# The delta rule's inverse: the mirrored update of each level by a transpose of the update's copy instead of a third product

## The chip, the cores and the metric

The kernel runs on one core of a Trainium2 chip. Time is device time in microseconds, the median of several executions. PE is TensorE, DVE VectorE, ACT ScalarE, POOL GpSimd, SP SyncE; PSUM is where PE writes, SBUF the working memory.

## What is computed

A stack of layers over 256 tokens with a width of 2048, all in fp32. The third layer has, beside other heads, eight heads of a gated delta rule. Cut to what matters, over the tokens of one head:

```python
kb = kc * bc[..., None]
L = jnp.where(tril & ~eye, jnp.einsum('bhncd,bhnsd->bhncs', kb, kc) * decay, 0.0)
rhs = jnp.concatenate([vc * bc[..., None], kb * jnp.exp(gc)[..., None]], axis=-1)
sol = lax.linalg.triangular_solve(L + eye, rhs, left_side=True, lower=True, unit_diagonal=True)
```

The kernel has no triangular solve. It treats each head as two blocks of 128 tokens, builds the inverse of each unit lower triangular 128x128 block (I + L) by doubling, and uses products with it for the rest. Level 0 is the inverse of the 2x2 blocks on the diagonal, I - L. Each of the levels 1 to 6 joins neighbouring blocks of size w = 2, 4, ... 64: the off-diagonal part is minus (inverse of the later block) times (L between them) times (inverse of the earlier one).

## The kernel before

**Streams.** One program per engine, written out by hand, with semaphores between them. The bulk is projections: weights come by DMA from SP in tiles of 128x2048, each in two pieces of 1024 columns. Each piece is split by ACT (L659, the high part) and DVE (L1487, the low part) into two tiles for which PE has fast passes; PE then multiplies it with the activations. ACT and DVE stay up to four pieces ahead (`ahead`, L444). Other work is written as generators, put in at *ticks* (L426): two for every piece, after its first and its second half. A `yield` ends a step, and `rate` says how many steps there are per tick: 5/6 for half 0 of the delta rule, later 7/8. In ACT's and DVE's programs (`proj`, L459) the split of a piece to come stands before the first tick of each piece. Each engine runs strictly in the order of its program. Evictions of a projection block stand after the last tick of its last piece.

**The delta rule** (`gdn`, one generator per engine, L1198 on ACT, L2325 on DVE, L3242 on PE) runs twice, for the halves H = 0 and 1 of four heads each. The names: `Tm` and `Tt` hold the inverses and their transposes, 512 columns (four heads) for each of two token blocks; `LM` is L with the level's mask, made by POOL (`inverse_masks`, L592); `Mx` holds copies; `DT` (`l3_dt`, 1536 columns) is free scratch by then, `LM` is its first third, `Two` its second.

One level, before:
- lm, PE L3330: four products, LM times the current inverse (a *mixed* view that takes one block of Tm and one of Tt). ACT copies the result to `Mx` (mx, L1273).
- ACT also copies the mixed inverse into `Two` (mix, L1269), after DVE has finished the level before.
- newm, PE L3336: four products Two times Mx. And right behind it new, PE L3340: four products with the operands exchanged, which give the transposed update.
- DVE subtracts newm's result (tn, L2438) and new's (tt, L2445) from the mixed views, straight from PSUM.

The next lm needs tn; the next mix needs tt. In the steps of the generators, lm stands in one step, newm and new in the next. ACT's mix and mx stand in newm's step, ahead of it, and both of DVE's subtractions in the step of the next lm. After level 6 PE makes u0 (L3346), which needs tt6, then lu and u1, a step each. While the inverse of half 0 is built, projection blocks of half 1's inputs run, whose results DVE evicts in pairs (L1708 two reductions, L1713 a product); beside half 1's there is a block evicted by ACT with a change of table (L795).

The transposes that are in this layer already (L3308, L3315) are PE instructions with the identity as moving operand.

Of the kernel before, what the change touches and what calls it, by code (L numbers as in the profile page):

```python
# [11 lines left out]
ACT = mybir.ActivationFunctionType  # L12
# [99 lines left out]
def later(ap, h):  # L112

    return ap.rearrange("p (m n) -> p m n", n=2 * h)[:, :, h:2 * h]
# [6 lines left out]
def mixed(a, b, h):  # L121

    n = a.shape[1]
    return bass.AP(a.tensor, a.offset, [list(a.ap[0]), [2 * h, n // (2 * h)], [b.offset - a.offset + h, 2], [1, h]])
# [12 lines left out]
class Bank:  # L137


    def __init__(self, i, n, t):  # L140
# [5 lines left out]
    "lru_act": ("l1_r", "l1_i", "l1_tanh", "l1_ln", "l1_a", "l1_root", "lam_exp", "lam_ln", "l1_exp"),  # L146
    "gates_act": ("l2_gelu_u", "l2_gelu_v", "l2_silu_g", "gla_gate", "gd_gate", "hg_gate", "hg_sig", "gla_exp", "gla_ln",
                  "hg_ln", "lb_exp"),
    "gdn_act": ("gd_mix", "gd_decay", "gd_ln", "gd_mx", "gd_out", "gd_root", "gd_silu", "gd_sq", "gd_tm", "gd_u", "conv0"),
    "copied_act": ("l2_al", "l3_small", "l4_small", "l4_gl", "cmp_kc", "cmp_silu", "cmp_vc", "small"),  # L150
    "head_squares": ("hn_sq", "gate_sq"),
    "lru_dve": ("l1_conv", "l1_half", "l1_iu", "l1_neg", "l1_scan", "l1_u", "l1_y", "l1_zero", "lam", "lb"),
# [492 lines left out]
class Scalar(Lane):  # L645
# [552 lines left out]
    def gdn(self, H):  # L1198
        m, e = self.m, self.e
        qk, sm, DT, Tm, Tt, U = m.l3_qk, m.l3_sm, m.l3_dt, m.l3_tm, m.l3_tt, m.l3_mx  # L1200
        if H:
            yield from self.conv(1)
        self.silu_part(H, 2)
        yield
        yield
        if H == 0:
            bsv = sm[:, :, 32:48]
            self.wait_ge("small_T")
            b = self.bank("small_T")
            e.activation(bsv, b.t[:, 0:128].rearrange("p (a n) -> p a n", a=2)[:, :, 0:16], ACT.Copy).then_inc(  # L1210
                *self.up("small", 0, frees=[b]))
            self.sq_turned = ("small_T",)
            self.ln_set()
            e.activation(m.cell(8, "ea"), m.c("a_log", 0, 8), ACT.Exp).then_inc(*self.up("small", 1))
            self.wait_ge("small", 0)
            e.activation(sm[:, :, 8:16], bsv[:, :, 8:16], ACT.Exp, scale=-1.0).then_inc(*self.up("small", 2))
            yield
            self.wait_ge("small_v", "abs")
            e.activation(sm[:, :, 16:24], sm[:, :, 16:24], ACT.Exp, scale=-1.0).then_inc(*self.up("small", 3))
            self.wait_ge("small", 3)  # L1220
            e.activation(sm[:, :, 16:24], sm[:, :, 16:24], ACT.Ln, bias=1.0).then_inc(*self.up("small", 4))
        else:
            self.ln_set()
        for hh in range(0, 4, 2):
            yield
        if H == 0:
            yield
            self.wait_ge("small_sum")
            b = self.bank("small_sum")
            e.activation(sm[:, :, 24:32], b.t[:, 0:16].rearrange("p (a n) -> p a n", a=2), ACT.Copy).then_inc(  # L1230
                *self.up("small", 5, frees=[b]))
            yield
        for now in skew(4, 3):
            for s, g in now:
                dst = DT[:, (g % 3) * 512:(g % 3) * 512 + 512]
                if s == 0:
                    x2 = qk[:, 2 * g:2 * g + 2, :].rearrange("p c n -> p (c n)")
                    self.wait_ge("gd_silu", H, g // 2)
                    if g >= 3:
                        self.wait_ge("gd_unit", H, g - 3)  # L1240
                    e.activation(dst, x2, ACT.Square).then_inc(*self.up("gd_sq", H, g))
                if s == 2:
                    self.wait_ge("gd_ss", H, g)
                    b = self.bank("gd_ss", H, g)
                    e.activation(dst, b.t, ACT.Ln, bias=m.cst[:, C_EPS:C_EPS + 1]).then_inc(
                        *self.up("gd_ln", H, g, frees=[b]))
                    self.wait_ge("gd_ln", H, g)
                    e.activation(dst, dst, ACT.Exp, scale=-0.5).then_inc(*self.up("gd_root", H, g))
            yield
        for now in skew(4, 3):  # L1250
            yield
        self.wait_ge("gd_kb", H, 3)
        e.activation(DT, DT, ACT.Exp).then_inc(*self.up("gd_decay", H))
        yield
        for now in skew(8, 2):
            yield
        yield
        for g in range(2):
            self.wait_ge("gd_tT", H, g)
            b = self.bank("gd_tT", H, g)  # L1260
            e.activation(Tm[:, g * 512:(g + 1) * 512], b.t, ACT.Copy).then_inc(*self.up("gd_tm", H, 0, g, frees=[b]))
        for level in range(1, 7):
            yield
            w = 1 << level
            if level == 1:
                self.wait_ge("gd_tm", H, 0, 1)
            else:
                self.wait_ge("gd_tt", H, level - 1)
            e.activation(DT[:, 512:1024].rearrange("p (m c n) -> p m c n", c=2, n=w), mixed(Tm[:, 512:1024], Tt[:, 0:512], w),  # L1269
                         ACT.Copy).then_inc(*self.up("gd_mix", H, level))  # L1270
            self.wait_ge("gd_lm", H, level)
            b = self.bank("gd_lm", H, level)
            e.activation(U[:, 0:512], b.t, ACT.Copy).then_inc(*self.up("gd_mx", H, level, frees=[b]))  # L1273
            yield
        yield
        self.wait_ge("gd_u0", H)
        b = self.bank("gd_u0", H)
        e.activation(U[:, 0:512], b.t, ACT.Copy).then_inc(*self.up("gd_u", H, 0, frees=[b]))
        yield
        yield  # L1280
        self.wait_ge("gd_u1", H)
        b = self.bank("gd_u1", H)
        e.activation(U[:, 512:1024], b.t, ACT.Copy).then_inc(*self.up("gd_u", H, 1, frees=[b]))
        self.f.add("mid")
        yield
        for tt in range(2):
            self.wait_ge("gd_o", H, tt)
            b = self.bank("gd_o", H, tt)
            e.activation(m.l3_vb[:, tt, :], b.t, ACT.Copy).then_inc(*self.up("gd_out", H, tt, frees=[b]))
        yield from self.headnorm(f"gd{H}", m.l3_vb, 4, 128, DT, ("gd_out", H, 1))  # L1290
        self.ends(f"gd{H}")
# [187 lines left out]
class Vector(Lane):  # L1479
# [845 lines left out]
    def gdn(self, H):  # L2325
# [95 lines left out]
                            *self.up("gd_l2", H, frees=[b]))  # L2421
            yield
        yield
        a, b = slice(0, 512), slice(512, 1024)
        for level in range(1, 7):
            yield
            yield
            w = 1 << level
            two = lambda ap: ap.rearrange("p (m c n) -> p m c n", c=2, n=w)
            bk = self.bank("gd_newm", H, level)  # L2430
            if level == 1:
                self.wait_ge("gd_tm", H, 0, 1)
            self.wait_ge("gd_newm", H, level)
            if level < 6:
                T, P = mixed(Tm[:, a], Tt[:, b], w), two(bk.t)
            else:
                T, P = later(Tt[:, b], w), later(bk.t, w)
            e.tensor_tensor(T, T, P, SUB).then_inc(*self.up("gd_tn", H, level, frees=[bk]))  # L2438
            bk = self.bank("gd_new", H, level)
            self.wait_ge("gd_new", H, level)  # L2440
            if level < 6:
                T, P = mixed(Tm[:, b], Tt[:, a], w), two(bk.t)
            else:
                T, P = later(Tt[:, a], w), later(bk.t, w)
            e.tensor_tensor(T, T, P, SUB).then_inc(*self.up("gd_tt", H, level, frees=[bk]))  # L2445
        yield
        yield
        bk = self.bank("gd_lu", H)
        self.wait_ge("gd_lu", H)
# [208 lines left out]
class Tensor(Lane):  # L2658
# [583 lines left out]
    def gdn(self, H):  # L3242
# [74 lines left out]
        yield  # L3317


        LM, Two = m.l3_dt[:, 0:512], m.l3_dt[:, 512:1024]  # L3320
        for level in range(1, 7):
            w = 1 << level
            bk = self.take("ps", "gd_lm", H, level)
            self.wait_ge("gd_mask", H, level)
            if level == 1:
                self.wait_ge("gd_tm", H, 0, 1)
            else:
                self.wait_ge("gd_tn", H, level - 1)
            for h in range(4):
                t = self.mm(bk.t[:, hs(h)], inst(LM, h), mixed(inst(Tm, h), inst(Tt, 4 + h), w), start=h == 0)  # L3330
            t.then_inc(*self.up("gd_lm", H, level))
            yield
            self.wait_ge("gd_mx", H, level)
            bk = self.take("ps", "gd_newm", H, level)
            for h in range(4):
                t = self.mm(bk.t[:, hs(h)], inst(Two, h), inst(Mx, h), start=h == 0)  # L3336
            t.then_inc(*self.up("gd_newm", H, level))
            bk = self.take("ps", "gd_new", H, level)
            for h in range(4):
                t = self.mm(bk.t[:, hs(h)], inst(Mx, h), inst(Two, h), start=h == 0)  # L3340
            t.then_inc(*self.up("gd_new", H, level))
            yield
        bk = self.take("ps", "gd_u0", H)
        self.wait_ge("gd_tt", H, 6)
        for h in range(4):
# [334 lines left out]
```

## Time and profile before

| | us |
|---|---|
| median of 3 executions | 3354.71 |
| lowest, highest | 3354.18, 3355.12 |
| the profiled execution, its own time | 3355.44 |
| its span, first to last instruction | 3353.7 |
| PE busy | 3308.8 (99%) |
| DVE busy | 1985.0 (59%) |
| ACT busy | 1569.4 (47%) |
| POOL busy | 67.1 (2%) |
| mean granted clock of PE | 0.998 |

One execution is profiled, and rows show its instructions with start and duration. Consecutive matmuls overlap, so the time that a group takes from PE is read from starts, not from the sum of durations. A row of a timeline may merge instructions of the same kind (x8 is eight of them). The bracket at a row's end is how long the engine sat idle before it and what ended that.

### The profile page before, as it was taken

To read this page: it belongs to the slowest core of one execution; us is meant where nothing else is said; L and a number is where in the kernel's file an instruction comes from. 1 tells how busy PE (TensorE), PEld (TensorE's weight loads), DVE (VectorE), ACT (ScalarE), POOL (GpSimd) and SP (SyncE) were. 2 spreads that over 40 slices of the span, in tenths; PEclk is the share of its full clock that TensorE was granted. 3 is DMA by queue.
4 is the path that set the end of the run, shared out by engine and by line. 5 is a ranking of instruction groups with operands and counts; after the bars stand their busy time and mean duration, and the time that the engine had idled before them with its cause. 6 is when DMAs were issued, how large, how long until landed. Compare 5 with 4: busy or idle time off the path is not lost.

```text
span 3353.7 us, 40646 instructions
## 1 busy us (share of the span) xinstructions
PE 3308.8 (99%) x16752; PEld 2797.8 (83%) x16752; DVE 1985.0 (59%) x2603; ACT 1569.4 (47%) x2166; POOL 67.1 (2%) x67
## 2 busy tenths in 40 slices
PE   8999999999999999999999999999999999999998
PEld 8888888888889888778888888888888788888887
DVE  5875665575766857674444444574677654444455
ACT  4573444454553544454444444453455544444443
POOL 0000000000001010000000000000000000000000
PEclk9999999999999999999999999999999999999999
DMA  6454445455443434455555545554323555545544
GB/s 256 153 209 183 175 145 196 173 192 185 173 169 126 157 120 152 162 182 193 190 186 203 188 177 200 188 205 181 139 101 133 193 189 188 196 181 200 190 178 160
DMA packets 83352, 592.50 MB, mean 177 GB/s; under 512 B 9248, under 2 KB 9760, under 8 KB 12512
## 3 DMA queue, kind: packets, MB, share of 16 engines
q1 hardware_dynamic: 80880, 576.24, 47.2%
q0 software_dynamic: 2288, 13.67, 1.1%
q8 instruction: 132, 2.16, 0.3%
q14 instruction: 52, 0.43, 0.0%
HBM read 587.77 MB, written 2.10 MB: 176 GB/s over the span
## 4 chain that ended last, share of the span: by engine, by line
PE 92%; DVE 4%; ACT 2%; issue 1%; DMA 0%; POOL 0%; POOLq 0%; SPq 0%; DVEq 0%; ACTq 0%
PE ps L2678 90%; DVE wlo L1487 1%; ACT whi L659 1%; PE ps L3499 1%; DVE l L2305 0%; PE ps L2828 0%; ACT sq L669 0%; DVE xres L1770 0%; ACT l4s L1409 0%; PE ps L3474 0%; DVE l L1850 0%; DVE xx L1623 0%; DVE l L1851 0%; DMA raw<-in_ev_in 0%; PE ps L2928 0%
## 5 line engine op out<-in xcount | busy, mean ns | idle before, releaser
L1487 DVE TENSOR_TENSOR wlo<-raw,whi 128x1024 fp32r<-128x1024 f32 x1091 | 1309.6, 1220 | 878.7 <-ACT whi L659 877.3
L2678 PE MATMUL ps<-whi,xx 128*128 128x512 f32 x5184 | 1654.5, 394 | 3.3 <-DVE xx L1623 1.9
L659 ACT ACTIVATE whi<-raw 128x1024 fp32r<-128x1024 f32 x1091 | 1131.9, 1055 | 909.7 <-PE ps L2678 803.8
L2678 PEld LDWEIGHTS ps<-whi,xx 128*128 128x128 f32 x5184 | 974.1, 188 | 206.5 <-DVE wlo L1487 5.5
L2678 PE MATMUL ps<-wlo,xx 128*128 128x512 f32 x2592 | 1009.7, 390 | 0.0
L2678 PE MATMUL ps<-xx,whi 128*128 128x512 f32 (+3 forms) x2464 | 782.5, 375 | 2.2 <-DVE xx L1510 2.1
L2678 PE MATMUL ps<-xx,wlo 128*128 128x256 f32 x2160 | 606.8, 281 | 0.0
L2678 PEld LDWEIGHTS ps<-wlo,xx 128*128 128x128 f32 x2592 | 487.8, 188 | 95.0
L2678 PEld LDWEIGHTS ps<-xx,whi 128*128 128x128 f32 (+2 forms) x2464 | 440.3, 186 | 85.8 <-DVE wlo L1487 2.8
L2678 PEld LDWEIGHTS ps<-xx,wlo 128*128 128x128 f32 x2160 | 405.8, 188 | 3.2 <-issue 1.9
L2678 PE MATMUL ps<-whi,fhh 128*128 128x512 f32 x704 | 274.7, 390 | 0.0
L2678 PE MATMUL ps<-whi,fhl 128*128 128x512 f32 x704 | 274.0, 389 | 0.0
L2678 PE MATMUL ps<-wlo,fhh 128*128 128x512 f32 x704 | 273.9, 389 | 0.0
L2678 PEld LDWEIGHTS ps<-whi,fhl 128*128 128x128 f32 x704 | 132.2, 188 | 27.7
L2678 PEld LDWEIGHTS ps<-whi,fhh 128*128 128x128 f32 x704 | 132.2, 188 | 27.3
L2678 PEld LDWEIGHTS ps<-wlo,fhh 128*128 128x128 f32 x704 | 132.2, 188 | 27.0
L2678 PEld LDWEIGHTS ps<-l 128*128 128x128 f32 x656 | 84.6, 191 | 14.5 <-DVE l L1863 7.0
L2678 PE MATMUL ps<-l 128*128 128x128 f32 (+1 forms) x656 | 89.8, 283 | 5.8 <-ACT l L832 4.8
L1424 ACT ACTIVATE fhh<-ps 128x512 fp32r<-128x512 f32 x44 | 26.3, 598 | 141.4 <-PE ps L3499 141.4
L537 POOL TENSOR_TENSOR st<-st,cst 128x4 f32<-128x4 f32 (+2 forms) x27 | 32.2, 1195 | 2533.2 <-DVE st L1494 2533.1
L2609 DVE TENSOR_TENSOR fhl<-ps,fhh 128x512 fp32r<-128x512 f32 x44 | 30.4, 692 | 85.0 <-ACT fhh L1424 85.0
L1409 ACT ACTIVATE l4s<-l4s,st 128x128 f32<-128x128 f32 (+2 forms) x96 | 37.9, 396 | 74.3 <-DVE st L2579 74.3
(360 smaller groups left out, 1691.3 us busy)
## 6 DMA issues: line engine op xcount, KB each, us to landing
raw<-in_ffn_gu SPq DMA_DIRECT2D x176, 1024.0 KB, 4.8
raw<-in_ffn_down SPq DMA_DIRECT2D x88, 1024.0 KB, 4.8
raw<-in_ab_in SPq DMA_DIRECT2D x64, 1024.0 KB, 4.8
raw<-in_ev_in SPq DMA_DIRECT2D x63, 1024.0 KB, 4.8
raw<-in_od_in SPq DMA_DIRECT2D x48, 1024.0 KB, 4.8
raw<-in_nsa_in SPq DMA_DIRECT2D x40, 1024.0 KB, 4.8
raw<-in_ev_out SPq DMA_DIRECT2D x16, 1024.0 KB, 4.7
raw<-in_od_out SPq DMA_DIRECT2D x16, 1024.0 KB, 4.8
```

Of the source, the lines that this page charges most:

```text
L537: self.e.tensor_tensor(m.cell(n, "rs", *key), m.cell(n, "var", *key), m.cst[:, C_HALF:C_HALF + n], ALU.pow).then_inc(*self.up("rstd", *key))
L659: self.e.activation(m.hi[i % NSPLIT][:, 0:w], m.raw[t % NRAW][:, off:off + w], ACT.Copy).then_inc(*self.up("hi", i))
L1409: e.activation(ap, ap, ACT.Exp, bias=mx[:, i:i + 1], accum_out=den[:, i:i + 1]).then_inc(*self.up("l4_exp", it, i))
L1424: self.e.activation(m.f_hh[:, 4 * i:4 * i + 4, tt * 128:(tt + 1) * 128], b.t.rearrange("p (c n) -> p c n", c=4), ACT.Copy).then_inc(*self. ...
L1487: self.e.tensor_tensor(m.lo[i % NSPLIT][:, 0:w], m.raw[t % NRAW][:, off:off + w], m.hi[i % NSPLIT][:, 0:w].bitcast(F32), SUB).then_inc(*se ...
L2609: self.e.tensor_tensor(m.f_hl[:, 4 * i:4 * i + 4, tt * 128:(tt + 1) * 128], b.t.rearrange("p (c n) -> p c n", c=4), hs.bitcast(F32), SUB). ...
L2678: return self.e.matmul(out, l, r, start=start, stop=stop, skip_group_check=True)
L3499: t = self.e.transpose(b.t[:, i * 128:(i + 1) * 128], m.f_t[(2 * nb + tt) % 4][:, i * 128:(i + 1) * 128], m.ident)
```

## The change

The third product (new) is gone. ACT copies newm's result from PSUM to SBUF (nm, into the last third of `DT`, called `Nm`). PE turns that copy with four transposes into the bank that new's product went to. DVE's tn reads the copy instead of the PSUM bank, and tt reads the transposes. The steps are arranged anew: PE's transposes of a level stand in front of the next level's lm, in one step; nm stands in that step on ACT, and so does tn on DVE; tt stands one step later. After level 6 the transposes and u0 stand in one step of PE. The number of steps is the same on each engine.

```diff
--- before.py
+++ after.py
@@ -146,7 +146,7 @@
     "lru_act": ("l1_r", "l1_i", "l1_tanh", "l1_ln", "l1_a", "l1_root", "lam_exp", "lam_ln", "l1_exp"),
     "gates_act": ("l2_gelu_u", "l2_gelu_v", "l2_silu_g", "gla_gate", "gd_gate", "hg_gate", "hg_sig", "gla_exp", "gla_ln",
                   "hg_ln", "lb_exp"),
-    "gdn_act": ("gd_mix", "gd_decay", "gd_ln", "gd_mx", "gd_out", "gd_root", "gd_silu", "gd_sq", "gd_tm", "gd_u", "conv0"),
+    "gdn_act": ("gd_mix", "gd_decay", "gd_ln", "gd_mx", "gd_nm", "gd_out", "gd_root", "gd_silu", "gd_sq", "gd_tm", "gd_u", "conv0"),
     "copied_act": ("l2_al", "l3_small", "l4_small", "l4_gl", "cmp_kc", "cmp_silu", "cmp_vc", "small"),
     "head_squares": ("hn_sq", "gate_sq"),
     "lru_dve": ("l1_conv", "l1_half", "l1_iu", "l1_neg", "l1_scan", "l1_u", "l1_y", "l1_zero", "lam", "lb"),
@@ -1272,6 +1272,9 @@
             b = self.bank("gd_lm", H, level)
             e.activation(U[:, 0:512], b.t, ACT.Copy).then_inc(*self.up("gd_mx", H, level, frees=[b]))
             yield
+            self.wait_ge("gd_newm", H, level)
+            b = self.bank("gd_newm", H, level)
+            e.activation(DT[:, 1024:1536], b.t, ACT.Copy).then_inc(*self.up("gd_nm", H, level, frees=[b]))
         yield
         self.wait_ge("gd_u0", H)
         b = self.bank("gd_u0", H)
@@ -2421,29 +2424,28 @@
                             *self.up("gd_l2", H, frees=[b]))
             yield
         yield
-        a, b = slice(0, 512), slice(512, 1024)
+        a, b, Nm = slice(0, 512), slice(512, 1024), DT[:, 1024:1536]
+        yield
         for level in range(1, 7):
-            yield
             yield
             w = 1 << level
             two = lambda ap: ap.rearrange("p (m c n) -> p m c n", c=2, n=w)
-            bk = self.bank("gd_newm", H, level)
             if level == 1:
                 self.wait_ge("gd_tm", H, 0, 1)
-            self.wait_ge("gd_newm", H, level)
+            self.wait_ge("gd_nm", H, level)
             if level < 6:
-                T, P = mixed(Tm[:, a], Tt[:, b], w), two(bk.t)
+                T, P = mixed(Tm[:, a], Tt[:, b], w), two(Nm)
             else:
-                T, P = later(Tt[:, b], w), later(bk.t, w)
-            e.tensor_tensor(T, T, P, SUB).then_inc(*self.up("gd_tn", H, level, frees=[bk]))
+                T, P = later(Tt[:, b], w), later(Nm, w)
+            e.tensor_tensor(T, T, P, SUB).then_inc(*self.up("gd_tn", H, level))
             bk = self.bank("gd_new", H, level)
+            yield
             self.wait_ge("gd_new", H, level)
             if level < 6:
                 T, P = mixed(Tm[:, b], Tt[:, a], w), two(bk.t)
             else:
                 T, P = later(Tt[:, a], w), later(bk.t, w)
             e.tensor_tensor(T, T, P, SUB).then_inc(*self.up("gd_tt", H, level, frees=[bk]))
-        yield
         yield
         bk = self.bank("gd_lu", H)
         self.wait_ge("gd_lu", H)
@@ -3317,7 +3319,7 @@
         yield
 
 
-        LM, Two = m.l3_dt[:, 0:512], m.l3_dt[:, 512:1024]
+        LM, Two, Nm = (m.l3_dt[:, i * 512:i * 512 + 512] for i in range(3))
         for level in range(1, 7):
             w = 1 << level
             bk = self.take("ps", "gd_lm", H, level)
@@ -3335,11 +3337,12 @@
             for h in range(4):
                 t = self.mm(bk.t[:, hs(h)], inst(Two, h), inst(Mx, h), start=h == 0)
             t.then_inc(*self.up("gd_newm", H, level))
+            yield
+            self.wait_ge("gd_nm", H, level)
             bk = self.take("ps", "gd_new", H, level)
             for h in range(4):
-                t = self.mm(bk.t[:, hs(h)], inst(Mx, h), inst(Two, h), start=h == 0)
+                t = tr(bk.t[:, hs(h)], inst(Nm, h), m.ident)
             t.then_inc(*self.up("gd_new", H, level))
-            yield
         bk = self.take("ps", "gd_u0", H)
         self.wait_ge("gd_tt", H, 6)
         for h in range(4):
```

## Rows read from the trace of the kernel before

**Rows 1.** The page, part 4: the chain that ended last.
```profile
PE 92%; DVE 4%; ACT 2%; issue 1%; DMA 0%; POOL 0%; POOLq 0%; SPq 0%; DVEq 0%; ACTq 0%
```

**Rows 2.** Timeline of PE: start us, us, engine, line, operation, tiles, count.
```profile
1042.32 1.03 PE L3315 MATMUL ps<-cst,l 128*128 128x128 f32 x8
1043.11 0.48 PE L2678 MATMUL ps<-xx,whi 128*128 128x512 f32 x1
1051.58 1.05 PE L2678 MATMUL ps<-l 128*128 128x128 f32 x8
1052.38 0.47 PE L2678 MATMUL ps<-xx,whi 128*128 128x512 f32 x1
1053.85 1.95 PE L2678 MATMUL ps<-l 128*128 128x128 f32 x16
1055.55 0.48 PE L2678 MATMUL ps<-xx,whi 128*128 128x512 f32 x1
```

**Rows 3.** Windows: busy us of each engine, granted clock, DMA share, GB/s.
```profile
1042.00:1044.00 2.00, 2.00 (x17) 1.87 (x16) 1.23 (x2) 1.04 (x3) 1.82 (x1) 1.00 0.00 0
```

**Rows 4.** Timeline of ACT, levels 1 and 2 of half 0.
```profile
1042.96 1.09 ACT L1261 ACTIVATE l<-ps 128x512 f32<-128x512 f32 x2 [2.86 <-PE ps L3315]
1047.67 1.05 ACT L659 ACTIVATE whi<-raw 128x1024 fp32r<-128x1024 f32 x1
1051.08 0.63 ACT L1269 ACTIVATE l<-l 128x512 f32<-128x512 f32 x1 [2.36 <-DVE l L2445]
1052.66 0.60 ACT L1273 ACTIVATE l<-ps 128x512 f32<-128x512 f32 x1 [0.95 <-PE ps L2678]
```

**Rows 5.** Timelines of DVE, and of POOL (one row), half 0.
```profile
1050.36 0.69 DVE L2445 TENSOR_TENSOR l<-l,ps 128x512 f32<-128x512 f32 x1
1051.84 1.29 DVE L1708 TENSOR_REDUCE l<-ps 128x256 f32<-128x512 f32 x2 [0.79 <-PE ps L2678]
1052.71 1.31 POOL L592 TENSOR_TENSOR l<-l,cst 128x512 f32<-128x512 f32 x1 [4.19 <-PE ps L2678]
1053.16 1.40 DVE L1713 TENSOR_TENSOR l<-l,rb 128x512 f32<-128x512 f32 x1
1054.49 1.21 DVE L1487 TENSOR_TENSOR wlo<-raw,whi 128x1024 fp32r<-128x1024 f32 x1
1055.62 0.67 DVE L2438 TENSOR_TENSOR l<-l,ps 128x512 f32<-128x512 f32 x1
```

**Rows 6.** Timelines of ACT (first row) and DVE, level 3 of half 1.
```profile
1205.41 1.05 ACT L659 ACTIVATE whi<-raw 128x1024 fp32r<-128x1024 f32 x1
1206.50 1.23 DVE L1487 TENSOR_TENSOR wlo<-raw,whi 128x1024 fp32r<-128x1024 f32 x1 [2.02 <-ACT whi L659]
```

**Rows 7.** Timelines of ACT, DVE and PE, end of half 1's inverse.
```profile
1223.18 1.28 ACT L795 ACT_TABLE_LOAD   x1
1225.63 2.01 ACT L659 ACTIVATE whi<-raw 128x1024 fp32r<-128x1024 f32 x2
1228.19 0.41 DVE L2445 TENSOR_TENSOR l<-l,ps 128x256 f32<-128x256 f32 x1
1228.75 0.46 PE L2678 MATMUL ps<-l 128*128 128x128 f32 x2 [0.33 <-DVE l L2445]
```

**Rows 8.** PE's longer waits elsewhere (timeline), and windows behind two of them.
```profile
1369.07 1.13 PE L2678 MATMUL ps<-l 128*128 128x128 f32 x8 [2.52 <-ACT l L832]
2388.02 0.63 PE L3474 MATMUL ps<-cst,l4s 128*128 128x128 f32 x4 [2.17 <-DVE l4s L2596]
2480.16 0.63 PE L3474 MATMUL ps<-cst,l4s 128*128 128x128 f32 x4 [3.60 <-DVE l4s L2596]
1370.00:1375.00 5.00, 4.82 (x26) 3.86 (x26) 4.08 (x6) 1.58 (x2) 0.00 (x0) 1.00 0.25 103
2390.00:2395.00 5.00, 5.00 (x28) 4.46 (x28) 3.17 (x12) 2.34 (x7) 0.00 (x0) 0.78 0.00 0
2480.00:2485.00 5.00, 4.84 (x19) 4.09 (x20) 2.21 (x9) 1.40 (x6) 0.00 (x0) 0.66 0.36 149
```

## Prediction

> **What bounds the kernel now.** The page first. The chain that ended last is 92% PE [rows 1]: time is won or lost where PE's own stream gets shorter, or where PE is made to wait. So I read the stretch in which the inverse is built (1044 to 1076 us for half 0, 1191 to 1229 us for half 1) in PE's timeline, and then asked of ACT and DVE when they deliver, because the change moves work onto their chain.
>
> PE's stream there is projection work with inverse groups put in at ticks. Four fp32 products of 128x128 are 8 instructions and take 0.80 us from their start to the next projection matmul; eight products (16 instructions) take 1.70 us; from one group to the next there is one tick, 1.47 us of projection [rows 2]. Where the pattern leaves a tick out it is two ticks, some 2.9 us. In the two stretches together PE waits once for the inverse, 0.33 us, before u0 of half 1 [rows 7]. The inverse is therefore hidden today, and its price is its PE time.
>
> **What is taken from PE.** Per level the third product (8 instructions) goes: 1.70 - 0.80 = 0.90 us. Four transposes of the same 128x128 fp32 size come: eight transposes (L3315) are 8 instructions, not 16, and take 0.79 us to the next matmul [rows 2], so four take 0.40. Gain 0.50 a level, 12 levels: 6.0 us. That is 0.18% and about the most that the change can give.
>
> The Trainium skill speaks against that price: "TensorE: Matmul & The Clock Gate", Part 4, says that with transposes the full clock doesn't engage. Here it was granted in full around the eight transposes, 1.00 from 1042 to 1044 us [rows 3], so trace and page differ; by the page the four would cost up to 0.80. This is the fourth rival below.
>
> **What is put on the chain.** Before, one PE group gave both products, DVE subtracted both, and ACT had a whole tick for its merged copy (L1269). After, the mirror is made in series: newm on PE, copy on ACT (nm), transposes on PE, subtraction tt on DVE, merged copy (mix) and copy of lm (mx) on ACT, next newm on PE. Durations and delays, from rows:
> - PE group of four products to ACT's start: 1.08 (1051.58 to 1052.66); of the first four transposes to ACT's start: 0.64 (1042.32 to 1042.96) [rows 2, 4]. For DVE I take the same.
> - ACT: copy from PSUM 0.60, mix 0.63, split (L659) 1.05; the next one starts 0.10 before the end (two splits take 2.01 together). The new copy has the form of L1273, so 0.60 [rows 4, 7].
> - DVE: subtraction 0.68, next start after 0.60; split (L1487) 1.22, next start after 1.13. ACT to DVE 0.04, DVE to ACT 0.03, DVE to PE 0.14 (1228.60 to 1228.75); ACT to PE I take as that too [rows 4, 5, 6, 7]. tn now reads two SBUF operands instead of one from PSUM. No such tn is in the trace; the nearest rows are L1713, 0.69 on such operands elsewhere, and 1.40 here where POOL's mask ran from 52.71 to 54.02 [rows 5]. So tn costs between 0 and 0.7 more. I take 0: the mask starts 1.13 after lm and takes 1.31, tn starts 3.99 after lm.
>
> That last choice agrees with the Trainium skill ("SBUF — State Buffer", Who interferes with whom): a VectorE instruction with two SBUF inputs and a GpSimd one that reads SBUF exclude each other. If they met at each level, twelve tn would come 0.7 later, up to 8 us on top of the sum; the starts above say that they don't meet.
>
> **Where the splits lie.** ACT and DVE run the inverse's steps in program order with one weight split per two ticks. A split is either between the nm/tn step and the next mix/tt step (place P), or after mx and before nm/tn (place Q). The trace shows which: of one piece, ACT's split (1047.67) lies before mix2 (1051.08) and DVE's (1054.49) after tt1 (1050.36) and before tn2, so P, with the eviction of a pair block in front of it on DVE [rows 4, 5]; in half 1 the piece that ACT splits at 1205.41, after mx3, DVE splits at 1206.50, before tn3, so Q [rows 6]. I went through all twelve levels like this. P: to level 2, 3 and 6 and the end of half 0; to level 2 and 3 and the end of half 1. The rest are Q. The order of DVE's steps is the diff's: tt moves one step later, which is past the split wherever the place is P.
>
> I laid the before order out with these numbers from the first lm of each half; starts of PE groups come within 0.25 us of the trace. The after order, laid out the same way, gives these waits of PE:
> - Half 0, newm of level 2. From tr1's start: newm2 is due after 0.40 + 0.80 + 1.47 = 2.67. DVE starts the pair eviction at 0.26, holds it 2.65 (1051.84 to 1054.49), then the split 1.13, so tt starts at 4.04; tt 0.69, mix 0.03 + 0.53, mx 0.60, 0.14 to PE: 6.03. **PE waits 3.36.** If the port falls the other way the eviction takes 2.0 (wait 2.7), if it is held to the mask's end 3.0 (wait 3.7).
> - Half 1, newm of level 2 (plain P). From newm1: copy at 1.08, ACT split at 1.58, DVE split at 2.67, tt at 3.80, mix at 4.51, mx at 5.04 to 5.64, newm2 can start at 5.78; due at 0.80 + 1.47 + 0.40 + 0.80 + 1.47 = 4.94. Wait 0.84. Half 0, level 6, also P but with two ticks earlier in the level: 0.61. Level 3 of both halves is P with two ticks: none.
> - Q levels: DVE's split ends just before tn; lm waits under 0.1, three times (0.16 in half 0, 0.09 in half 1).
> - Half 0, u0. tr6 and u0 now stand in one step, and u0 needs tt6, one step later on DVE and past a split. From newm6: tt6 starts at 3.80 as above, takes 0.41 (half size) and 0.14 to PE, 4.35; due 0.80 + 1.47 + 0.40 = 2.67. Wait 1.68.
> - Half 1, u0. nm6 stands on ACT behind a table load (1223.18), two evictions and the first of two splits (1225.63). In these rows' times nm6 runs from 1226.59 to 1227.19, the second split to 1228.14, DVE's to 1229.4, tt6 starts at 1229.31, and u0 can start at 1229.86. PE has newm6 at 1223.30 (it follows mx6, as the table load does on ACT) and is due with tr6 after 0.80 and two ticks, 1227.0; it waits 0.3 for nm6, is at u0 at 1227.73 and waits 2.13 [rows 7].
>
> Half 0: 3.36 + 0.61 + 1.68 + 0.16 = 5.81. Half 1: 0.84 + 0.09 + 0.30 + 2.13 = 3.36. Together 9.17, less the 0.33 that was there: 8.8 of new waiting against 6.0 of saved work, **+2.8 us**. What is queued behind the waiting instruction is all of PE's projection work; nothing later takes it up, since every later PE wait hangs on PE-fed work. ACT and DVE are four pieces ahead with their splits, some 11 us, so PE doesn't run dry of weights. SP's queue and POOL's are not moved.
>
> **The clock.** A long wait can have a second price. After PE's waits of 2.17 and 3.60 us (2388.02, 2480.16) the granted clock fell to its lower level of 1.2 GHz for some us: mean 0.66 over 2480 to 2485, so 5 x 0.34 = 1.7 us lost; after the other 0.78 over 2390 to 2395, 1.1 lost, with a part in the five before. After the wait of 2.52 (1369.07) it stayed at 2.4 GHz (1.00 over 1370 to 1375) [rows 8]. Of the new waits the 3.36 one is nearest to the 3.60: I take one fall, +1.7. The two near 2 us are between the precedents. Sum: **+4.5 us**, bounds 0 (no fall) and 5.1 (three) for the clock.
>
> The profiled execution took 3355.44 (span 3353.7), 0.73 over the median of 3354.71. So 3359.9 by its measure, and 3359.2 as median.
>
> **Rivals.**
> 1. The waits don't come: ACT is busy for 47% of the span and DVE for 59%, their starts shift, and the cover holds at each step. For it: PE's wait today is 0.33 [rows 7]. Against it: the plain P chain is 5.78 long where 4.94 is there, from measured durations. Gives -6.0: 3348.7. Chance 0.10, with 0.06 more for a cover that holds in part, between -5 and +1.
> 2. The waits come and the clock holds, as after the 2.52 wait: +2.8, 3357.5; +2.2 if DVE gets its port before the mask. Chance 0.20.
> 3. The slow side: the clock falls after each of the waits of 3.36, 1.68 and 2.13, 1.7 us each. For it: the 2.17 precedent. Against: the 2.52 one. +2.8 + 5.1 = +7.9, 3362.6. It decides from the third fall on. Chance 0.17.
> 4. The transposes run at half rate, for a reason that lies in their kind: 0.40 more a level, 12 x 0.40 = 4.8 on top of 2.8: 3362.3. The granted clock of 1.00 around eight of them speaks against it [rows 3]. Chance 0.02. (It is the rule of the Trainium skill's clock page named above.)
>
> **How the numbers follow.** Forecast (computed waits, one fall, own range 3357 to 3361.2): 0.45. With the rivals (0.10, 0.06, 0.20, 0.17, 0.02) that is 1.00. A measurement of this kernel can tell about 0.2%, 6.7 us. Faster by more than that would need more than all of the saved PE time: 0.02. Slower by more: rival 3 mostly, rival 4 and the forecast's tail: 0.20. Within: 0.78. The range leaves out rival 1 and the far ends: 3352 to 3363.5.
>
> **What would show it.** In the profile after: 48 transposes on PE in the two stretches at 0.10 us each; waits of PE on ACT L1273 of about 3.4 us at level 2 of half 0 and 0.9 at level 2 of half 1; waits on DVE's second subtraction of 1.7 and 2.2 before u0; a lower granted clock behind the first. If level 2 of half 0 shows no wait of over 2 us, my placing of tt behind the pair eviction is wrong, and with it the sign. If waits are there but add up to under 6 us, the chain's delays are over-sized.

## The result and the profile after

The changed kernel takes 3361.42 us (median of 14 executions, 3359.79 to 3362.23), the kernel before, beside it, 3354.35 (14 executions). The ratio is 1.0021, its 95% interval 1.0014 to 1.0028: slower by 7.1 us (4.7 to 9.4). The forecast was 3359.2, +4.5: 2.2 too low as a time, 2.6 as a difference.

In what follows a number behind a name is the level: lm2 is the lm of level 2, tr1 stands for the four transposes of level 1, and so on.

The page of the changed kernel, parts 1 and 4 (busy time of each engine, and the chain that ended last):

```profile
span 3358.4 us, 40562 instructions
PE 3306.7 (98%) x16704; PEld 2793.5 (83%) x16704; DVE 1985.8 (59%) x2603; ACT 1575.5 (47%) x2178; POOL 66.9 (2%) x67
...
PE 92%; DVE 5%; ACT 2%; issue 1%; DMA 0%; POOL 0%; POOLq 0%; SPq 0%; DVEq 0%; ACTq 0%
```

PE is busy for 2.1 us less than before and the span is 4.7 us longer; DVE has one point more of the chain. PE's waits from 1020 to 1245 us, the stretch of both inverses (in total, times, longest):

```profile
PE ps L2680 <- ACT l L1273: 4.2, 3, 3.4
PE ps L2680 <- DVE l L2448: 3.5, 2, 2.0
PE ps L3262 <- ACT l L1196: 0.5, 1, 0.5
```

L1273 is mx, L2448 is tt. Before, there was one such wait, of 0.33 [rows 7]. The last of these lines is older than the inverse and is in both kernels. PE's timeline at the new waits; the first four rows answer to [rows 2], the last two to the end of half 1 in [rows 7]:

```profile
1048.91 0.60 PE L3344 MATMUL ps<-cst,l 128*128 128x128 f32 x4
1049.35 1.06 PE L2680 MATMUL ps<-l 128*128 128x128 f32 x8
1055.26 1.01 PE L2680 MATMUL ps<-l 128*128 128x128 f32 x3 [3.44 <-ACT l L1273]
1059.69 1.06 PE L3344 MATMUL ps<-cst,l 128*128 128x128 f32 x4
...
1078.78 1.13 PE L2680 MATMUL ps<-l 128*128 128x128 f32 x8
1081.57 1.16 PE L2680 MATMUL ps<-l 128*128 128x128 f32 x8 [0.27 <-ACT l L1273]
1083.95 0.60 PE L3344 MATMUL ps<-cst,l 128*128 128x128 f32 x4
1086.05 1.13 PE L2680 MATMUL ps<-l 128*128 128x128 f32 x8 [1.49 <-DVE l L2448]
...
1202.57 1.06 PE L2680 MATMUL ps<-l 128*128 128x128 f32 x8
1205.55 1.16 PE L2680 MATMUL ps<-l 128*128 128x128 f32 x8 [0.53 <-ACT l L1273]
...
1230.90 0.66 PE L3344 MATMUL ps<-cst,l 128*128 128x128 f32 x4
1233.57 1.13 PE L2680 MATMUL ps<-l 128*128 128x128 f32 x8 [2.01 <-DVE l L2448]
```

Four transposes take 0.44 us to the next group (1048.91 to 1049.35). Behind the wait of 3.44 the same four take 0.85 (1059.69 to 1060.54): the clock is down. Windows of the changed kernel (granted clock third from the end), behind the 3.44 wait and behind the 2.01 one:

```profile
1050.00:1055.00 5.00, 1.82 (x12) 1.36 (x10) 4.02 (x4) 0.91 (x2) 1.28 (x1) 0.95 0.15 25
1055.00:1060.00 5.00, 4.75 (x18) 4.36 (x19) 1.75 (x2) 1.75 (x3) 0.00 (x0) 0.50 0.46 188
1060.00:1065.00 5.00, 5.00 (x32) 4.67 (x31) 2.08 (x3) 2.06 (x3) 1.30 (x1) 0.87 0.00 0
...
1234.00:1238.00 4.00, 4.00 (x27) 3.55 (x26) 0.99 (x2) 1.54 (x2) 0.00 (x0) 1.00 0.45 190
```

The clock was at its lower level (0.50, which is 1.2 GHz) for the whole window from 1055 to 1060 and a part of its neighbours, and in full behind u0 of half 1. What made newm2 late is seen on DVE and ACT. First DVE, then POOL (one row), then ACT, answering to [rows 4, 5]:

```profile
1048.40 0.69 DVE L2440 TENSOR_TENSOR l<-l 128x512 f32<-128x512 f32 x1 [3.88 <-ACT l L1277]
1049.18 1.29 DVE L1711 TENSOR_REDUCE l<-ps 128x256 f32<-128x512 f32 x2
1050.51 1.81 DVE L1716 TENSOR_TENSOR l<-l,rb 128x512 f32<-128x512 f32 x1
1052.24 1.21 DVE L1490 TENSOR_TENSOR wlo<-raw,whi 128x1024 fp32r<-128x1024 f32 x1
1053.38 0.68 DVE L2448 TENSOR_TENSOR l<-l,ps 128x512 f32<-128x512 f32 x1
...
1050.49 1.28 POOL L592 TENSOR_TENSOR l<-l,cst 128x512 f32<-128x512 f32 x1 [3.74 <-PE ps L2680]
...
1054.09 0.63 ACT L1269 ACTIVATE l<-l 128x512 f32<-128x512 f32 x1 [4.85 <-DVE l L2448]
1054.62 0.58 ACT L1273 ACTIVATE l<-ps 128x512 f32<-128x512 f32 x1
```

tr1 runs from 1048.91 to about 1049.5, yet its subtraction (L2448) starts at 1053.38: the pair eviction (L1711, L1716) and the split (L1490) stand in front of it. ACT has waited 4.85 us for it, and mx, whose input lm2 was there at about 1050.4, stands behind mix.

**One measure for all kernels.** Profiled executions differ by up to 1.8 us ahead of the inverse: the first lm starts at 1044.24 after and at 1046.02 before, and PE's first wait, for a transfer of the input that the change doesn't touch, took 5.4 and 6.7. So beside medians I give the time from the first lm of half 0 to the end of the span, less the same of before (3353.7 - 1046.02 = 2307.7). After: 3358.4 - 1044.24 = 2314.2, **+6.5**.

| kernel | median, us | less before's | ratio, 95% interval | first lm to end, less before's |
|---|---|---|---|---|
| after | 3361.42 | +7.1 | 1.0021 (1.0014 to 1.0028) | +6.5 |
| e1, tt in front | 3350.21 | -3.8 | 0.9988 (0.9979 to 0.9997) | -3.5 |
| e2, and u0 later | 3348.74 | -5.3 | 0.9985 (0.9977 to 0.9994) | -5.0 |
| e3, gain alone | 3349.7 | -4.3 | 0.9989 (0.998 to 0.9997) | -5.1 |
| e4, order alone | 3361.03 | +7.0 | 1.0022 (1.0013 to 1.0031) | +6.0 |
| e5, wait filled, transposes | 3358.76 | +4.5 | 1.0014 (1.0005 to 1.0023) | +5.4 |
| e6, wait filled, products | 3358.36 | +4.1 | 1.0014 (1.0005 to 1.0023) | +5.4 |
| e7, one tt in front | 3354.28 | 0.0 | 1.0001 (0.9992 to 1.0009) | 0.0 |

The kernel before took 3354.0 beside e1 to e4 (33 executions) and 3354.24 beside e5 to e7 (27); the experiments have 11 each. One of the 33 took 6739 us, counts as a slow run and is left out of the ratios; what made it so is not known. The two columns of differences agree within 1.3 us throughout.

### The profile page after: what moved, and what is told of

It reads as the page before. It is cut to its first block, busy times and chain, and to the rows that moved or that the text cites. A ratio compares the mean times of both kernels' runs of the same rounds, so it can differ in the third digit from the quotient of the medians.

```text
span 3358.4 us, 40562 instructions
## 1 busy us (share of the span) xinstructions
PE 3306.7 (98%) x16704; PEld 2793.5 (83%) x16704; DVE 1985.8 (59%) x2603; ACT 1575.5 (47%) x2178; POOL 66.9 (2%) x67
## 4 chain that ended last, share of the span: by engine, by line
PE 92%; DVE 5%; ACT 2%; issue 1%; DMA 0%; POOL 0%; POOLq 0%; SPq 0%; DVEq 0%; ACTq 0%
PE ps L2680 90%; DVE wlo L1490 2%; ACT whi L659 1%; PE ps L3502 1%; DVE l L2308 0%; PE ps L2830 0%; ACT sq L669 0%; DVE xres L1773 0%; PE ps L3477 0%; DVE l L1853 0%; ACT l4s L1412 0%; DVE l L1711 0%; DVE l L1854 0%; DVE xx L1626 0%; PE ps L2930 0%
## 5 line engine op out<-in xcount | busy, mean ns | idle before, releaser
L1490 DVE TENSOR_TENSOR wlo<-raw,whi 128x1024 fp32r<-128x1024 f32 x1091 | 1309.7, 1220 | 876.1 <-ACT whi L659 874.7
L659 ACT ACTIVATE whi<-raw 128x1024 fp32r<-128x1024 f32 x1091 | 1132.1, 1055 | 909.7 <-PE ps L2680 804.5
L2680 PE MATMUL ps<-l 128*128 128x128 f32 (+1 forms) x560 | 81.0, 288 | 13.3 <-ACT l L832 4.8
L2680 PEld LDWEIGHTS ps<-l 128*128 128x128 f32 x560 | 74.4, 194 | 22.5 <-DVE l L1866 7.1
```

The source lines that it names most:

```text
L659: self.e.activation(m.hi[i % NSPLIT][:, 0:w], m.raw[t % NRAW][:, off:off + w], ACT.Copy).then_inc(*self.up("hi", i))
L1490: self.e.tensor_tensor(m.lo[i % NSPLIT][:, 0:w], m.raw[t % NRAW][:, off:off + w], m.hi[i % NSPLIT][:, 0:w].bitcast(F32), SUB).then_inc(*se ...
L2680: return self.e.matmul(out, l, r, start=start, stop=stop, skip_group_check=True)
```

## The experiments

**Theory.** The PE work saved is worth what its rows say; the loss is made by the new order of steps, which puts a split, and once a pair eviction too, in front of tt, and by the clock that falls behind the longest wait. **Rivals:** the chain is too long in itself, whatever the order (copy and transposes in series); or the transposes are slow on PE.

### e3: the gain alone

```diff
--- before.py
+++ e3
             for h in range(4):
-                t = self.mm(bk.t[:, hs(h)], inst(Mx, h), inst(Two, h), start=h == 0)
+                t = tr(bk.t[:, hs(h)], inst(Two, h), m.ident)
```

The order and the operations of before, with four transposes of `Two` in place of the third product. The mirrored update is left out: what tt subtracts is the transpose of another tile.

> The kernel before, with its order, but the four products of new replaced by four transposes of Two: the mirrored update is left out of the computation (what is turned is not the update), all counts and waits are those of the kernel before. It measures what PE saves. Theory: 12 times (0.90 - 0.44) = 5.5 us, 3348.9, with no new wait. Rival (a transpose is dearer than its rows say, or the clock falls with it): under 3 us saved, and a granted clock under 1.00 in the stretch.

Measured: -4.3, and by the trace -5.1. PE's newm and new of level 1 in the kernel before (first row), then e3's timeline of level 1 and its waits over the stretch:

```profile
1048.38 1.95 PE L2678 MATMUL ps<-l 128*128 128x128 f32 x16
...
1047.53 1.05 PE L2678 MATMUL ps<-l 128*128 128x128 f32 x8
1048.42 0.60 PE L3340 MATMUL ps<-cst,l 128*128 128x128 f32 x4
1050.26 0.94 PE L2678 MATMUL ps<-l 128*128 128x128 f32 x7
...
PE ps L2678 <- DVE l L2445: 0.8, 1, 0.8
```

From newm to the next lm it is 2.73 us (1047.53 to 1050.26), where before took 3.20 (1048.38 to 1051.58 [rows 2]): 0.47 a level. In half 1 it is 0.45 (2.71 against 3.16), so some 5.5 in twelve. The wait before u0 of half 1 grew from 0.33 [rows 7] to 0.76: with PE sooner at u0, the same tt6 is later against it. So 5.5 - 0.4 = 5.1. The rival of slow transposes falls: the transposes are worth nearly what was said.

### e4: the order alone

The order of the steps of after, but with the third product, without the copy, and tn from PSUM as before.

```diff
--- after.py
+++ e4
@@ ACT
-            self.wait_ge("gd_newm", H, level)
-            b = self.bank("gd_newm", H, level)
-            e.activation(DT[:, 1024:1536], b.t, ACT.Copy).then_inc(*self.up("gd_nm", H, level, frees=[b]))
@@ DVE
-            self.wait_ge("gd_nm", H, level)
+            bk = self.bank("gd_newm", H, level)
+            self.wait_ge("gd_newm", H, level)
             if level < 6:
-                T, P = mixed(Tm[:, a], Tt[:, b], w), two(Nm)
+                T, P = mixed(Tm[:, a], Tt[:, b], w), two(bk.t)
...
@@ PE
             yield
-            self.wait_ge("gd_nm", H, level)
             bk = self.take("ps", "gd_new", H, level)
             for h in range(4):
-                t = tr(bk.t[:, hs(h)], inst(Nm, h), m.ident)
+                t = self.mm(bk.t[:, hs(h)], inst(Mx, h), inst(Two, h), start=h == 0)
```

> The changed kernel's order with the third product kept: new is again four products of Mx and Two, put where the transposes stand, no copy on ACT, tn reads PSUM again. Same result as the reference. Theory: the order costs as much without the copy: PE waits about 3.3 us at level 2 of half 0, 0.3 at level 6, 0.8 and 2.0 at u0, the clock falls once for about 3 us; 8.3 us over the kernel before, 3362.7. Rival (the copy through ACT is what makes PE wait): no wait over 1 us, and the time of the kernel before within 1.5 us.

Measured: +7.0, with nothing of the copy or of the transposes in it. PE's waits over the stretch, and windows of the clock behind the longest and behind the older wait on L832 [rows 8]:

```profile
PE ps L2678 <- ACT l L1273: 3.0, 1, 3.0
PE ps L2678 <- DVE l L2446: 2.4, 2, 1.8
...
1055.00:1060.00 5.00, 3.12 (x12) 2.93 (x13) 1.69 (x4) 2.06 (x3) 0.00 (x0) 0.66 0.58 210
...
1375.00:1380.00 5.00, 3.80 (x16) 3.20 (x17) 4.10 (x7) 2.08 (x3) 0.00 (x0) 0.75 0.59 213
1380.00:1385.00 5.00, 5.00 (x26) 4.22 (x25) 3.41 (x7) 2.14 (x4) 0.00 (x0) 0.91 0.34 93
```

5.4 of waits plus 1.7 of clock (5 x 0.34) is 7.1, and from the first lm to u1 of half 1 the trace has 7.4 more than before. The order costs this much without the series of copy and transposes, and the rival falls. The 8.3 expected was too much: the fall of the clock was put at about 3 us and cost 1.7. And e3 with e4, -4.3 and +7.0, do not add up to after's +7.1: their sum is +2.7. After waits 7.7 in these rows where e4 waits 5.4, and its clock costs 2.8 (e5, below) where e4's costs 1.7: 3.4 of the 4.4 that are missing. So much of what the shorter groups save on PE comes back as waiting and lower clock, since they also cover less. The second fall, at 1375, lies behind a wait of 2.53; its like in the kernel before, 2.52, left the clock at 1.00 [rows 8]; in the same execution the fall at 2390 of [rows 8] is missing. Falls elsewhere in the kernel come and go from one execution to the next.

### e1: tt in front of the split and the eviction

```diff
--- after.py
+++ e1
@@ DVE
             bk = self.bank("gd_new", H, level)
-            yield
             self.wait_ge("gd_new", H, level)
...
             e.tensor_tensor(T, T, P, SUB).then_inc(*self.up("gd_tt", H, level, frees=[bk]))
+            yield
```

DVE makes tt right behind tn, and then ends its step. Copy and transposes stay.

> The changed kernel with one step undone: DVE's second subtraction (tt) stands right behind the first (tn) again, as in the kernel before, so in front of the pair eviction and the split. Same result as the reference. Theory (the loss is tt's place in DVE's queue, and the clock that its longest wait takes down): the waits of 3.4 us at level 2 of half 0 and of 0.5 and 0.3 at the other P places are gone, a wait of about 0.8 appears at the next lm of half 0 behind the eviction, u0 waits 0.75 and 1.0 instead of 1.5 and 2.0, no fall of the granted clock in the stretch; 3.1 us under the kernel before, 3351.3. Rival (the copy and the serial chain through it cost the time, wherever tt stands): the waits stay within 1 us of the changed kernel's, 3359 or more.

Measured: -3.8, a swing of 11 us (by the trace 10) from the place of one `yield`. Waits of PE over the stretch, and DVE's level 1:

```profile
PE ps L2680 <- DVE l L2447: 1.5, 2, 0.9
...
1049.62 0.69 DVE L2447 TENSOR_TENSOR l<-l,ps 128x512 f32<-128x512 f32 x1 [0.46 <-PE ps L3344]
1050.22 1.28 DVE L1711 TENSOR_REDUCE l<-ps 128x256 f32<-128x512 f32 x2
1051.54 0.85 DVE L1716 TENSOR_TENSOR l<-l,rb 128x512 f32<-128x512 f32 x1
1052.32 1.21 DVE L1490 TENSOR_TENSOR wlo<-raw,whi 128x1024 fp32r<-128x1024 f32 x1
```

tt runs at 1049.62 and not at 1053.38, at the price of a DVE that stands 0.46 for the transposes. Three of the five waits (of the first two lines of after's) are gone; the two before u0 are left, 0.60 and 0.88, and behind neither did the clock fall (1.00 from 1075 to 1090 and from 1220 to 1255). The rival of a chain too long in itself falls too. One wait expected here, 0.8 at lm of level 3, did not come: I had the eviction at its long duration, but tt in front moved L1716 to 1051.54, near the end of POOL's mask, and it took 0.85.

### e2: and u0 one step later

```diff
--- e1
+++ e2
@@ PE
             t.then_inc(*self.up("gd_new", H, level))
+        yield
         bk = self.take("ps", "gd_u0", H)
@@ ACT
         yield
+        yield
         self.wait_ge("gd_u0", H)
@@ DVE
             yield
         yield
+        yield
         bk = self.bank("gd_lu", H)
```

> As e1_tt_early, and u0 with the steps behind it one step later on PE, ACT and DVE. Same result as the reference. Theory: no wait of PE before u0 in either half; another 1.7 us less than e1_tt_early, some 4.8 us under the kernel before, 3349.6. Rival (what u0's wait gives back is lost at the end of the inverse, where steps run out of ticks): the same time as e1_tt_early.

Measured: -5.3, by the trace -5.0: the best of all, 12.4 us under after. No wait of the inverse is left in the stretch; the one row is the older one:

```profile
PE ps L3264 <- ACT l L1196: 0.5, 1, 0.5
```

Copy and transposes stand in series here as in after, and of the 5.5 us saved 5.0 arrive.

### e7: only the pair eviction's tt

```diff
--- after.py
+++ e7
@@ DVE
             bk = self.bank("gd_new", H, level)
-            yield
+            if (H, level) != (0, 1):
+                yield
             self.wait_ge("gd_new", H, level)
...
+            if (H, level) == (0, 1):
+                yield
```

One of the twelve tt, the one that had the pair eviction in front of it.

> The changed kernel with a single tt, that of level 1 in half 0, put back in front of the pair eviction; the other eleven stay. Same result as the reference. Theory: this one place holds 3.6 us of delay and 3 us of lower clock; without both 6.6 us under the changed kernel, 3354.8, the kernel before within 1 us. The waits at u0 stay at 1.5 and 2.0. Rival (the loss is spread over all levels): 3359 or more.

Measured: 0.0, 7.1 under after (6.5 by the trace), where the long wait and its clock together were to be worth 6.6. In its windows the clock is 1.00 from 1045 to 1070, and the other waits are there unchanged:

```profile
PE ps L2683 <- DVE l L2449: 3.5, 2, 2.0
PE ps L2683 <- ACT l L1273: 0.8, 2, 0.5
...
1055.00:1060.00 5.00, 5.00 (x36) 4.58 (x35) 2.84 (x3) 2.42 (x4) 1.29 (x1) 1.00 0.51 202
```

### e5 and e6: the wait filled

The long wait is kept as it is, but PE works in it: 28 transposes of constants (e5) or 14 fp32 products of them, 28 instructions too (e6), into the bank that newm writes afterwards. So the wait's two prices, idle time and clock, come apart.

```diff
--- after.py
+++ e5
@@ PE
+            if (H, level) == (0, 2):
+                bk = self.take("ps", "gd_newm", H, level)
+                for i in range(28):
+                    tr(bk.t[:, hs(i % 4)], m.one, m.ident)
             self.wait_ge("gd_mx", H, level)
-            bk = self.take("ps", "gd_newm", H, level)
+            if (H, level) != (0, 2):
+                bk = self.take("ps", "gd_newm", H, level)
```

> The changed kernel, and in half 0 at level 2, ahead of the wait for mx, 28 transposes of constants into the bank that newm then overwrites; some 2.9 us of PE work in a wait of 3.6 us. Same result as the reference. It takes the idle time away and leaves the delay. Theory (the long idle time costs a second time, through the clock, about 3 us): the granted clock stays at 1.00 in the stretch, PE goes on at the same point, and the time is 3 us under the changed kernel's, 3358.4. Rival (only the delay costs): the changed kernel's 3361.4 within 1 us. By the rule of the Trainium skill's clock page on transposes the clock would fall all the same, and the time be 3361.4; in a sentence of its own, since the forecast above stands on rows.

```diff
--- e5
+++ e6
@@ PE
-                for i in range(28):
-                    tr(bk.t[:, hs(i % 4)], m.one, m.ident)
+                for i in range(14):
+                    self.mm(bk.t[:, hs(i % 4)], m.one, m.ident)
```

> As e5_wait_filled_transposes, with 14 fp32 products of constants (28 instructions, some 3.0 us) in place of the 28 transposes. Same result as the reference. Theory: the same as there, 3358.4, clock 1.00. If it matters of what kind the filling is, this one holds the clock and the transposes don't: 3358.4 here and 3361.4 there.

Measured: +4.5 and +4.1, so 2.6 and 3.0 under after. Of e5, PE's timeline and the windows over it and behind u0 of half 1:

```profile
1051.13 1.06 PE L2680 MATMUL ps<-l 128*128 128x128 f32 x8
1053.44 3.22 PE L3338 MATMUL ps<-cst 128*128 128x128 f32 x28
1057.03 1.16 PE L2680 MATMUL ps<-l 128*128 128x128 f32 x8 [0.38 <-ACT l L1273]
1059.42 0.60 PE L3349 MATMUL ps<-cst,l 128*128 128x128 f32 x4
1059.86 1.06 PE L2680 MATMUL ps<-l 128*128 128x128 f32 x8
...
1050.00:1055.00 5.00, 5.00 (x41) 4.72 (x40) 4.70 (x5) 1.02 (x2) 1.29 (x1) 1.00 0.01 3
1055.00:1060.00 5.00, 4.62 (x38) 4.21 (x36) 1.72 (x4) 2.66 (x4) 0.00 (x0) 1.00 0.55 210
...
1230.00:1235.00 5.00, 2.99 (x17) 2.45 (x18) 2.43 (x4) 2.06 (x3) 0.00 (x0) 0.88 0.63 210
1235.00:1240.00 5.00, 5.00 (x27) 4.53 (x26) 2.39 (x4) 0.42 (x2) 0.00 (x0) 0.78 0.02 3
```

From lm2 to newm2 it is 5.90 us, in after 5.91: the filling neither shortened nor lengthened the wait. From newm2 to tr2 it is 2.39 instead of 4.43, from tr2 to lm3 0.44 instead of 0.85, and from lm3 to newm3 3.72 instead of 4.05. All of half 0 (first lm to u1) takes 43.64 instead of 46.42: **2.8 us is what the lower clock cost**. The delay cost 3.6: lm2 to newm2 is 5.91 in after and 2.31 in e7. The medians say the same as these two profiled executions: 2.6 and 3.0 for the clock.

The half 1 of the same execution shows a surprise: behind its wait of 2.01, which after has in the same length, the clock fell. u0 to u1 took 6.19 us against 4.61, so 1.6 lost; in e6 6.22. That is why the trace gives only 1.1 under after where 2.8 was gained. It fell in the profiled executions of e5 and e6 and not in those of after and e7. That of e5 was the longest of its eleven, 3360.9 against the median of 3358.76, so the fall is hardly in all of them. What decides it is open; no run here separates the cases.

The Trainium skill ("TensorE: Matmul & The Clock Gate", Part 4) says that transposes don't engage the full clock. These rows disagree: with 28 transposes for 3.2 us as PE's only work the granted clock was 1.00, where it fell in after with PE idle in the same place, and 14 products in their place (e6) gave the same +5.4 by the trace.

## Why the prediction came out as it did

The sign, the places and the order of size were right. The result lies inside the range, but it is 0.2 above the upper end of what the forecast alone gave (3357 to 3361.2), and nearer to the third rival's 3362.6 than to 3359.2; only the rows tell the two apart. A difference beyond 6.7 us had been given a chance of 0.20; it is 7.1, with an interval that reaches to both sides of that bound. By the prediction's steps:

- **Saved PE time.** Expected 0.50 a level. Four transposes take 0.44 in the stream, not 0.40: halving the eight of [rows 2] left out what a group costs by itself. Saved 12 x (0.90 - 0.44) = 5.5 in place of 6.0.
- **newm of level 2, half 0.** Expected 3.36; lm2 to newm2 is 5.91 where 2.27 was due, so 3.64 (due is 0.80 + 1.47). The eviction's last instruction was taken at its length of before (L1713, 1.40), and it took 1.81 (L1716), as it began with POOL's mask and ended 0.5 after it. This is the branch named as "held to the mask's end" (3.7).
- **Level 6 of half 0 and level 2 of half 1.** Expected 0.61 and 0.84; 0.52 (2.79 from start to start against 2.27) and 0.71.
- **u0.** Expected 1.68 and 2.13; 1.66 (2.10 from tr6 to u0, less 0.44) and 2.23 (2.67 less 0.44). Before it, tr6 of half 1 came 0.08 late, not 0.30.
- **Waits in all.** Half 0: 3.64 + 0.52 + 1.66 = 5.82, expected 5.81. Half 1: 0.71 + 0.08 + 2.23 = 3.02, expected 3.36. Net of the 0.33 that is 8.5, expected 8.8. That half 0 agrees to 0.01 is luck: 0.28 more at level 2 stands against 0.09 and 0.02 less and against 0.16 of small waits at lm that the profile doesn't name. tn from SBUF took 0.70 at most in all twelve, as taken.
- **The clock.** This is the term that was mis-sized: one fall as expected, but 2.8 us and not 1.7. I took the loss of a five-microsecond window behind the 3.60 wait [rows 8] as the price of a fall. That reading was right for its own fall (the windows on both sides of it are at 1.00), but here the low stretch was twice as long. e5 shows what it cost.
- **A slip that changes nothing.** The stretch of half 0 is given as 1044 to 1076; in the trace of before its first lm starts at 1046.02 and u0 at 1081.63.

That gives 8.5 + 2.8 - 5.5 = +5.8, against +6.5 by the trace and +7.1 by the median. The 0.7 between is in no wait that the profile names: from the first lm to u1, half 0 is 6.3 longer where its terms give 5.9, and half 1 is 0.2 longer where they give -0.1. A part of it is in the groups that follow a wait, which last a little longer up to the next group: newm6 to tr6 of half 0 2.38 (2.27 in e1, without the wait), newm2 to tr2 of half 1 2.39 (2.28 in e1), u0 to lu of half 0 2.34 (2.26 before); and newm2 to tr2 of half 0 has 0.12 more in e5, the measure of the 2.8, than in e7. That is 0.4; the other 0.3 stays open. The median has 0.6 beyond that; clock falls behind u0 in other executions of after, at 1.6 each, would do it, but that is argued and not shown.

Of the rivals, the first (the waits don't come) is out by the rows. The second (the clock holds) is out: it fell behind the longest wait. The third (a fall behind each wait of 3.36, 1.68 and 2.13) did not happen in the profiled execution of after, but one of its falls, that behind the last wait, did in e5 and e6. The fourth is out by e3 and e5.

What the prediction did not ask is where the loss could be avoided. It treated "copy and transposes in series" and "tt one step later" as one chain. The experiments show that they are two things. With tt in front, e1 keeps 3.5 of the 5.5 that are saved, and 1.5 of the rest are the two waits before u0, which stands in one step with tr6. With u0 a step later (e2) 5.0 are kept, so the series by itself costs some 0.5. The new order costs 7 (e4).

On L1716 the Trainium skill ("SBUF — State Buffer", Who interferes with whom) states an exclusive lock between VectorE and GpSimd on a shared port. The trace agrees: 1.81 us beside a mask that runs from 1050.49 to 1051.77, 0.85 in e1 where only the last 0.3 of the mask overlaps it (mask from 1050.55, 1.29 long). In both, and in the 1.40 of [rows 5], the product ends 0.54 or 0.55 us after the mask does (1052.32, 1052.39 and 1054.56), whenever it began.

## What to carry to other kernels

Before trading PE work for a longer hand-over between engines, lay out not only the chain but what stands in front of each of its links in program order: here the same work is 3.8 us faster or 7.1 slower than before, depending on whether one subtraction of each level stands ahead of a weight split. Price a long wait of PE twice, once as idle time and once for the clock: filling the one of 3.4 us with work that nothing uses gave back 2.8 us though the delay stayed (e5). Small groups that share a place in the stream are better costed from a row of the same size than as a half of a larger one.

## What the runs showed of the hardware that was not expected

- Behind the 3.44 us wait PE's clock stayed at 1.2 GHz from about 1054.5 to 1061.3 us. By the windows of after that is 5 x (0.05 + 0.50 + 0.13) = 3.4 us, of which 2.8 were paid; the clock fell while PE was still idle (until 1055.26). The other falls whose windows are given here took half as much: 5 x 0.34 = 1.7 behind the longer wait of 3.60 [rows 8], 5 x (0.34 + 0.01) behind e4's of 2.97 (0.99 from 1060 to 1065), 5 x (0.25 + 0.09) behind its 2.53, 5 x (0.12 + 0.22) behind e5's of 2.01. The length of the idle time alone does not set the length of the low stretch.
- Waits of the same length were followed by different clocks: 2.01 us by 1.00 (after, e7) and by 0.88 and 0.78 (e5); the wait on L832 by 1.00 in the kernel before (2.52) and by 0.75 and 0.91 in e4 (2.53).
- The same product of DVE (L1716, L1713 before) takes 0.69 without POOL's mask, 0.85 over the mask's last 0.3 us, 1.40 and 1.81 when more of the mask lies over it. In e1 the other side paid: a mask that began at 1055.57, while DVE's split ran (from 1055.24, 1.22 long), took 2.04 instead of 1.29.
